# Two-layer diffusion backbone, one core: the token rows that layer 0 dispatches to its experts are transposed back from the modulated channels

## What is computed

```python
def modln(x, g, shift, scale):
    return rmsnorm(x, g) * (1 + scale) + shift
...
for l in range(DEPTH):                                  # DEPTH = 2
    sh_a, sc_a, gt_a, sh_f, sc_f, gt_f = jnp.split(mod, 6, axis=-1)   # mod = silu(c) @ w_mod[l] + b_mod[l]
    ...                                                 # attention part, x = x + gt_a * y
    h2 = modln(x, g_ffn[l], sh_f, sc_f)
    if need_ctx:                                        # layer 0: 512 tokens, layer 1: 256
        ...
        yt = hier_moe(toks, w_rg[l], b_rg[l], w_re[l], b_re[l], w_e_gate[l], w_e_up[l], w_e_down[l])
return rmsnorm(x, g_final)
```

## Time and profile before

| | us |
|---|---|
| median of 3 runs | 1371.19 (1368.15 to 1374.7) |
| the profiled execution, own time | 1368.83 |
| its span | 1366.6 |
| PE / DVE / ACT / POOL busy in the span | 1220.4 / 661.0 / 437.8 / 176.2 |
| mean granted clock of PE, share of full speed | 0.97 |
| router stage of layer 0, mod(0,5) to the first expert matmul | 474.6 to 526.6 |
| router stage of layer 1, the same | 1081.1 to 1117.0 |

### The profile page before, as it was taken

One profiled execution on the slowest core, in us unless ns is written; L12 is line 12 of the kernel. 1 busy time (PEld: TensorE's weight loads), 2 busy tenths in 40 slices (PEclk: granted clock), 3 DMA queues, 4 the chain that ended last, 5 costly groups with the idle time before them and its releaser, 6 DMA issues.

```text
span 1366.6 us, 22075 instructions
## 1 busy us (share of the span) xinstructions
PE 1220.4 (89%) x8916; PEld 930.6 (68%) x8916; DVE 661.0 (48%) x1506; ACT 437.8 (32%) x1028; POOL 176.2 (13%) x220
## 2 busy tenths in 40 slices
PE   4899888899998978899999789998998968889986
PEld 2788754688887947666666459865998845555652
DVE  1544686455346375422221285567767554233334
ACT  3533366433334440000100264346666510000001
POOL 1810000111013200100010311000101200000001
PEclk9999999999999989999999989999999889999997
DMA  9994145423324378999999995238565869999994
GB/s 353 318 353 144 62 152 188 125 93 93 95 90 185 114 270 346 360 418 415 407 388 375 403 222 158 101 131 280 161 184 184 321 255 418 418 416 415 387 373 168
DMA packets 132391, 353.26 MB, mean 258 GB/s; under 512 B 23214, under 2 KB 84902, under 8 KB 109121
## 3 DMA queue, kind: packets, MB, share of 16 engines
q1 hardware_dynamic: 118144, 317.69, 62.9%
q0 software_dynamic: 13008, 32.48, 6.9%
q10 hardware_dynamic: 1136, 1.66, 0.3%
HBM read 332.62 MB, written 28.88 MB: 265 GB/s over the span
## 4 chain that ended last, share of the span: by engine, by line
PE 78%; DVE 10%; issue 4%; DMA 4%; ACT 2%; POOL 0%; SPq 0%; DVEq 0%; POOLq 0%; ACTq 0%
PE banks L1030 33%; PE banks L1259 15%; PE banks L1273 8%; PE banks L1251 6%; PE banks L1198 4%; PE banks L967 2%; PE banks L1126 2%; PE banks L1141 2%; PE banks L1111 1%; DMA expert_rows<-arena,rows_u 1%; DMA ring<-in_w_in 1%; DMA ring<-in_w_mod 1%; PE banks L1223 1%; DVE arena L2387 1%; DVE arena L2355 1%
## 5 line engine op out<-in xcount | busy, mean ns | idle before, releaser
L2000 DVE TENSOR_TENSOR w_lo_r<-ring,w_hi_r 128x256 fp32r<-128x256 f32 x480 | 222.8, 474 | 239.9 <-ACT w_hi_r L1608 238.8
L1608 ACT ACTIVATE w_hi_r<-ring 128x256 fp32r<-128x256 f32 x480 | 197.4, 416 | 303.1 <-PE banks L1030 254.0
L1259 PE MATMUL banks<-ring,arena 128*64 128x256 f32 x2016 | 230.6, 381 | 28.1 <-issue 11.4
L1030 PE MATMUL banks<-h_hi_r,w_hi_r 128*128 128x512 f32 (+1 forms) x640 | 222.0, 347 | 6.5 <-DVE h_lo_r L1930 5.1
L1259 PEld LDWEIGHTS banks<-ring,arena 128*64 128x64 f32 x2016 | 161.3, 137 | 87.1 <-issue 36.1
L1030 PE MATMUL banks<-h_lo_r,w_hi_r 128*128 128x512 f32 (+1 forms) x640 | 220.4, 344 | 0.0
L1030 PE MATMUL banks<-h_hi_r,w_lo_r 128*128 128x512 f32 (+1 forms) x640 | 220.3, 344 | 0.0
L1030 PEld LDWEIGHTS banks<-h_hi_r,w_hi_r 128*128 128x128 f32 x640 | 123.0, 192 | 22.5 <-ACT arena L1578 5.0
L1030 PEld LDWEIGHTS banks<-h_hi_r,w_lo_r 128*128 128x128 f32 x640 | 122.9, 192 | 14.1
L1030 PEld LDWEIGHTS banks<-h_lo_r,w_hi_r 128*128 128x128 f32 x640 | 123.1, 192 | 13.8
L1273 PE MATMUL banks<-ring,att 128*64 128x512 f32 x424 | 119.4, 604 | 14.7 <-DVE att L2372 7.4
(11 more groups left out here) (269 smaller groups left out, 1734.2 us busy)
## 6 DMA issues: line engine op xcount, KB each, us to landing
ring<-in_w_e_gate SPq DMA_DIRECT2D x64, 1024.0 KB, 9.0
ring<-in_w_e_up SPq DMA_DIRECT2D x62, 1024.0 KB, 9.3
ring<-in_w_e_down SPq DMA_DIRECT2D x53, 1024.0 KB, 9.5
ring<-in_w_mod SPq DMA_DIRECT2D x48, 1024.0 KB, 6.3
ring<-in_w_in SPq DMA_DIRECT2D x38, 1024.0 KB, 5.5
expert_rows<-att POOLq DMA_DIRECT2D x23, 512.0 KB, 20.4
ring<-in_w_o SPq DMA_DIRECT2D x8, 1024.0 KB, 5.2
ring<-in_w_branch SPq DMA_DIRECT2D x8, 640.0 KB, 4.5
```

The source lines that it names most:

```text
L1030: ins = mm(out_ap, a, b, start=k == 0 and p_ == 0, stop=k == KD - 1 and p_ == 2)
L1259: ins = mm(banks[e * CAP:(e + 1) * CAP, bank, 0:DE], x[:, k, e * CAP:(e + 1) * CAP], w[:, k * DE:(k + 1) * DE], start=k == 0, stop=k == KD ...
L1608: fn(w_hi[:, u % AHEAD, :, :], chunk(key)[:, q * KU:(q + 1) * KU, :], ACT.Copy).then_inc(w_hi_ready, 1)
L2000: v.tensor_tensor(w_lo[:, u % AHEAD, :, :], chunk(key)[:, q * KU:(q + 1) * KU, :], w_hi[:, u % AHEAD, :, :].bitcast(F32), ALU.subtract).th ...
```

## The change

Six edits, all in the router stages and at the end:
1. Layer 0's second computation of the modulated rows goes away, with its four row stores, four broadcasts and DVE's two passes. PE transposes `hT` back instead (`turn_rows`: 8 transposes a tile; tiles 0 and 1 before mod(1,1), tiles 2 and 3 after `ranks`), and ACT copies each tile out twice (`htok`, `th_hi`). `hT` moves to tiles 0 to 7 of `arena`. Rows now have `hT`'s channel order, so `rest_rows` reads without stride.
2. `ffn_norm` on DVE does the statistics before mod_add(0,5) and before the column copies, which now stand in the middle of the scaling.
3. The router product is done in two halves: even blocks into PSUM partitions 0 to 35, odd ones into 64 to 99. ACT copies one, DVE the other; PE adds both while turning them, by matmuls with the identity.
4. `ranks` signals after the ranks and again after the counts, which get a bank of their own.
5. mod_add(1,1) stands ahead of `place`, mod_add(1,0) between two halves of `rest_rows`.
6. At the end the tiles go through RMSNorm one by one, and tile 1 is stored in two halves.

```diff
-        hT = [att[:, NTOK * k:NTOK * (k + 1)] for k in range(KD)]
+        hT = [arena[:, k, :] for k in range(KD)]
...
+        ROW_BANKS = [(3, 0), (4, 5), (3, 0), (4, 5)]
...
-                if l == 0:
-                    rows_out(0, 4)
-                    rows_out(0, 3)
                 merge(l)
-                if l == 0:
-                    pool.wait_ge(branch_done, 24)
-                    rows_in(0, 4, mod_scale, ffn_rows_in)
-                    rows_in(0, 3, mod_shift, ffn_rows_in)
...
-                    ins = mm(banks[0:NR, 0, 0:n], w_router[:, k, :], hT[k][:, 0:n], start=k == 0, stop=k == KD - 1)
+                    p0 = k % 2 * 64
+                    ins = mm(banks[p0:p0 + NR, 0, 0:n], w_router[:, k, :], hT[k][:, 0:n], start=k < 2, stop=k >= KD - 2)
                 ins.then_inc(lgT_done, 1)
                 pe.wait_ge(lgT_out, l + 1)
-                hold()
+                pe.wait_ge(lgT_out_dve, l + 1)
                 for tt in range(QT[l]):
-                    ins = turn(banks[:, 2, tt * NR:(tt + 1) * NR], lgT[:, tt * P:(tt + 1) * P], ident[0:NR, 0:NR])
+                    for half in range(2):
+                        ins = mm(banks[:, 2, tt * NR:(tt + 1) * NR], lgT[half][:, tt * P:(tt + 1) * P], ident[0:NR, 0:NR],
+                                 start=half == 0, stop=half == 1)
...
+            def turn_rows(tiles):
+
+                for tt in tiles:
+                    if tt >= 2:
+                        pe.wait_ge(th_hi_ready, tt - 1)
+                    for k in range(KD):
+                        ins = turn(banks[:, ROW_BANKS[tt][k // 4], k % 4 * P:(k % 4 + 1) * P], hT[k][:, tt * P:(tt + 1) * P], ident)
+                    ins.then_inc(h_rows, 1)
...
                 for u in range(1, nt):
-                    mm(banks[:, 1, u * NE:nt * NE], C["ones"], pairs[:, 0:(nt - u) * NE], start=False, stop=u == nt - 1)
+                    ins = mm(banks[:, 1, u * NE:nt * NE], C["ones"], pairs[:, 0:(nt - u) * NE], start=False, stop=u == nt - 1)
+                ins.then_inc(rank_done, 1)
                 for u in range(nt):
-                    ins = mm(banks[:, 1, 4 * NE:5 * NE], C["ones"], both[:, u, :], start=u == 0, stop=u == nt - 1)
+                    ins = mm(banks[:, 2, 8 * NE:9 * NE], C["ones"], both[:, u, :], start=u == 0, stop=u == nt - 1)
                 ins.then_inc(rank_done, 1)
...
                 pe.wait_ge(sel_ready, n + 1)
+                if l == 0:
+                    pe.wait_ge(th_hi_ready, 3)
...
+                    if l == 0:
+                        for tt in (2 * r, 2 * r + 1):
+                            act.wait_ge(h_rows, tt + 1)
+                            for dst in (htok[:, tt, :], th_hi[:, tt, :]):
+                                for half, b in enumerate(ROW_BANKS[tt]):
+                                    ins = fn(dst[:, half * 512:half * 512 + 512], banks[:, b, :], ACT.Copy)
+                            ins.then_inc(th_hi_ready, 1)
-                if l == 0:
-                    act.wait_ge(wo_done, 4 * nt)
-                    for tt in range(nt):
-                        act.wait_ge(h_rows, tt + 1)
-                        fn(th_hi[:, tt, :].rearrange("p (k s) -> p k s", k=KD),
-                           htok[:, tt, :].rearrange("p (s k) -> p k s", k=KD), ACT.Copy).then_inc(th_hi_ready, 1)
...
                 residual(l)
-                mod_add(*MOD_ROUTE[l][0])
                 ffn_norm(l)
                 if l:
-                    rest_rows(1)
+                    rest_rows(1, range(2))
                 route(l)
                 if l == 0:
-                    shift_rows()
+                    mod_add(*MOD_ROUTE[0][1])
                 place(l, False)
-                for k, sec in MOD_ROUTE[l][1:]:
-                    mod_add(k, sec)
                 if l == 0:
-                    rest_rows(0)
+                    rest_rows(0, range(2))
+                    mod_add(*MOD_ROUTE[0][2])
+                    rest_rows(0, range(2, 4))
...
+            for c in range(2):
+                gathered_row(0, c)
+            add_own(1, 0)
+            gathered_row(1, 0)
+            mean_square(2, 0)
+            gathered_row(1, 1)
+            add_own(1, 1)
             dve.wait_ge(g_in, 16)
+            final_scale(0)
+            mean_square(2, 1)
+            final_scale(1)
```

More of the change, by code:

```diff
@@ L361, in program @@
         g_col = sb("g_col", [P, DEPTH, KD])
-        mod_scale = [tile(0, 2), tile(4, 2)]
-        mod_shift = [tile(2, 2), tile(6, 2)]
         gate_bc = [gate_t[:, s, :] for s in range(2)]
@@ L407, in program @@
         g8 = att[:, 1280:1312].rearrange("p (t e) -> p t e", t=4)
-        lgT = att[0:NR, 3072:3072 + NTOK]
+        lgT = [att[0:NR, 3072 + NTOK * half:3072 + NTOK * (half + 1)] for half in range(2)]
         rope_t = att[:, 2304:2304 + 4 * SEQ].rearrange("p (a b) -> p a b", a=4)
@@ L1498, in _ @@
                 route(l)
+                if l == 0:
+                    turn_rows((0, 1))
                 for k, sec in MOD_ROUTE[l][1:2]:
@@ L1502, in _ @@
                 ranks(l)
+                if l == 0:
+                    turn_rows((2, 3))
                 for k, sec in MOD_ROUTE[l][2:]:
@@ L1710, in route @@
                 act.wait_ge(lgT_done, l + 1)
-                fn(lgT[:, 0:QN[l]], banks[0:NR, 0, 0:QN[l]], ACT.Copy).then_inc(lgT_out, 1)
+                fn(lgT[0][:, 0:QN[l]], banks[0:NR, 0, 0:QN[l]], ACT.Copy).then_inc(lgT_out, 1)
                 for r, (dst, src) in enumerate((
@@ L1845, in _ @@
                 fn(htok[:, tt, :], X[:, tt, :], ACT.Square, accum_out=stat[:, tt:tt + 1]).then_inc(sq_done, 1)
-            act.wait_ge(ms_ready, MS0[4] + 1)
-            fn(stat[:, 8:12], stat[:, 4:8], ACT.Sqrt).then_inc(std_ready, 1)
-            for tt in range(2):
-                act.wait_ge(fin_ready, tt + 1)
-                act.dma_start(out[0, tt * P:(tt + 1) * P, :], htok[:, tt, :]).then_inc(stored, 16)
-            act.wait_ge(stored, 32)
+                act.wait_ge(ms_ready, MS0[4] + tt + 1)
+                fn(stat[:, 8 + tt:9 + tt], stat[:, 4 + tt:5 + tt], ACT.Sqrt).then_inc(std_ready, 1)
+            act.wait_ge(fin_ready, 1)
+            act.dma_start(out[0, 0:P, :], htok[:, 0, :]).then_inc(stored, 16)
+            for half in range(2):
+                at = slice(512 * half, 512 * half + 512)
+                act.wait_ge(fin_ready, 2 + half)
+                act.dma_start(out[0, P:2 * P, at], htok[:, 1, at]).then_inc(stored, 16)
+            act.wait_ge(stored, 48)
         @block.vector
@@ L1955, in ffn_norm @@
                 v.reciprocal(stat[:, 12:16], stat[:, 8:12]).then_inc(f_rstd_ready, 1)
+                mod_add(*MOD_ROUTE[l][0])
                 dve.wait_ge(f_rstd_ready, l + 1)
                 for tt in range(nt):
+                    if tt == nt // 2:
+                        for n, (dst, bank) in enumerate(((f_mul, 6), (f_add, 7))):
+                            dve.wait_ge(f_cols_done, 2 * l + n + 1)
+                            v.tensor_copy(dst[:, :, :], banks[:, bank, 0:2 * KD].rearrange("p (k s) -> p k s", s=2))\
+                                .then_inc(f_col_ready, 1)
                     r = stat[:, 12 + tt:13 + tt]
@@ L1972, in ffn_norm, with rest_rows @@
                                         ALU.mult, ALU.add).then_inc(hT_dve, 1)
[L1973 to L1994 removed]
+            def rest_rows(l, tiles):
+                for tt in tiles:
+                    dve.wait_ge(th_hi_ready, QT0[l] + tt + 1)
+                    v.tensor_tensor(th_lo[:, tt, :], htok[:, tt, :], th_hi[:, tt, :].bitcast(F32), ALU.subtract).then_inc(th_lo_ready, 1)
             def split_w(key, q):
@@ L2166, in route @@
                 nt = QT[l]
+                dve.wait_ge(lgT_done, l + 1)
+                v.tensor_copy(lgT[1][:, 0:QN[l]], banks[64:64 + NR, 0, 0:QN[l]]).then_inc(lgT_out_dve, 1)
+                link(v.memset(g8[:, :, :], NEG))
                 dve.wait_ge(lg_done, l + 1)
-                link(v.memset(g8[:, :, :], NEG))
                 link(v.tensor_tensor(lg[:, 0:nt, :], banks[:, 2, 0:nt * NR].rearrange("p (t n) -> p t n", t=nt),
```

70 lines of the change are left out of this document (21 added, 49 removed).

## The result

| | before | changed |
|---|---|---|
| median, us | 1370.37 (14 runs) | 1363.46 (14 runs, 1359.36 to 1366.49) |
| ratio to before | 1 | 0.9945, 95% interval [0.993, 0.9959] |
| profiled execution, own time / span | 1368.83 / 1366.6 | 1366.03 / 1364.2 |
| router stage of layer 0: mod(0,5) to the first expert matmul | 52.0 | 42.7 |
| router stage of layer 1, the same | 35.9 | 37.9 |

The change is 6.9 us faster by the medians, 7.5 by the ratio (5.6 to 9.6 by its interval). The forecast was 11.7 won, at 1359.5. Everything ahead of mod(0,5), which the change leaves alone, took 2.16 us longer in it than in the profile before (476.75 against 474.59).

The account below looks back on a forecast made before the run. Bounds: PE, 78% of the chain, with gains where the chain leaves PE; layer 0's weight stream second. Terms 7.2 + 3.5 + 1.0 = 11.7 us gave 1359.5 from the median, own range 1355 to 1363, wider range 1353 to 1366.

Parts of the forecast that it names:

- Layer 0, 7.2: Layer 0's router stage and weight stream: 7.2 us won, taken between 6.7 and 7.6.
- Statistics first: Layer 0, before the router product: transposes wait only for the column copy, start 482.4 for 483.88, 1.5 us won.
- halves side by side: Layer 0's router product: two halves run two by two, 0.22 us a pass, ending at 491.7; 5.1 us won so far.
- the queue's next request: Layer 0's weight queue: next piece asked for at 522.7 instead of 530.33, data at 524.6 for 531.3, 6.7 us won.
- Layer 1, 3.5: Layer 1's router stage: earlier transposes and product, ranks not waiting for counts; 3.5 us won, bounds 2.5 and 4.5.
- Before they were hidden under the product, now they are late next: Layer 1: `th_hi` (2.01 us) and `rest_rows` (2.36) stand ahead of the router result's copies; DVE's copy at 1094.2.
- The end, 1.0: Final norm and store: last half row ready 0.7 us earlier, last store half as long; 1.0 us, bounds 0.4 and 1.6.
- Clock rival: Layer 0, router product to mod(1,1): clock falls to 1.2 GHz, layer 0 wins 3.7 us, time 1363; chance 0.15.
- Halves don't overlap: Router product still takes 7.0 us; layer 0 wins 3.7, layer 1 3.2, time 1363.3; chance 0.10.
- stream eats it: Weight waits up to 670 return all of layer 0's gain but 1.9 us; time 1364.8; chance 0.08.
- slower: PE stays at 1.2 GHz from router product to dispatch, layer 0 9.2 us late; time 1375.9; chance 0.04.
- Dispatch released by ACT's `th_hi`: Layer 0: ACT's 16 copies arrive last, ending tile 3 at 508.5; dispatch starts then instead of 514.58.

Follow-up runs that it names:

- two repeats: Changed kernel with 100 and 160 empty PE instructions, which the build dropped, so byte for byte the changed kernel; ratios to before 0.993 and 0.9931.
- l0_only: Changed kernel with its edits of layer 1 and of the end undone; ratio to before 0.9947, 7.3 us faster.
- pad100: Changed kernel plus 25 thin matmuls (100 instructions) at the first unit of layer 1's output projection; ratio to before 0.9938.
- pad200: Changed kernel plus 50 thin matmuls (200 instructions) at the first unit of layer 1's output projection; ratio to before 0.9916.
- pad200_copy: pad200 with layer 1's copies of the router result ahead of `th_hi` and th_lo, `rest_rows` behind `place`; ratio to before 0.989, median 1356.24 us.
- pad256: Changed kernel plus 64 thin matmuls (256 instructions, a whole block) at the first unit of layer 1's output projection; ratio to before 0.9925.
- tail_only: Kernel before with only edit 6, the norm tile by tile and last store in halves; ratio to before 0.9993, 1.0 us faster.
- before_pad: Kernel before plus 38 thin matmuls in layer 0's output projection and 26 in layer 1's; ratio to before 0.9994.
- turn_later: pad_both with layer 0's first 16 `turn_rows` transposes moved behind mod(1,1); ratio to before 0.9875.
- pad_both: pad200_copy, but with 38 thin matmuls in layer 0's output projection and 12 in layer 1's; ratio to before 0.9904.

## Why the forecast came out as it did

- **Sum.** 11.7 forecast, 6.9 measured (7.5 by the ratio; 9.6 and 9.5 in the two repeats). The measured time (1363.46) is in the range of 1353 to 1366, but 0.5 above the forecast's own range of 1355 to 1363. The number is in range by luck in part: one term of three, layer 1, brought nothing, and the range was wide enough for it.
- **Layer 0, 7.2: right.** l0_only gives 7.3. Statistics first, halves side by side, the memset ahead of the signal, `place` without `shift_rows` and the queue's next request all show as forecast. Inside, two sizes were off. The stage gained more: eight profiles with the same layer 0 code (the changed kernel, its two repeats, l0_only, pad100, pad200, pad200_copy, pad256) have 42.7 to 44.4, mean 43.4, against 52.0 and 52.1 for before and tail_only: 8.7 us, 7.6 forecast. The forecast had DVE pace the router product; in fact PE's own passes pace it (0.43 us each in either half), and it ends at 492.62, which is 490.5 on the axis of before, 1.2 ahead of the 491.7 forecast. And the kernel lost some behind the stage: the first expert's matmuls take 8.8 us, at a clock of 0.50 in part, in nine of the eleven profiles with the changed layer 0, and 7.13 in the three without. What lies between the first expert and mod(1,5) varies from 554.4 to 561.1 us over the profiles, so the rest of the difference can't be followed there.
- **Layer 1, 3.5: the term that failed.** "Now they start at 1087.0 ... The same edits let the product end at about 1092": the first half was right, and then came a wait that I had not named, for PE's own instructions. Against 35.88 (before), 34.99 (tail_only) and 35.84 (before_pad), mean 35.6, the four profiles with the gap in its old place have 37.94, 35.79, 36.30 and 35.60, mean 36.4: nothing won, some 0.8 us lost, which is within the spread of the single stages. With the code moved so that nothing is awaited, the stage is 32.7 (one profile, pad200) and 2.9 us are won, within my bounds of 2.5 to 4.5. There DVE's copy ends 13.2 us after mod(1,5) begins; the forecast's 1094.2 is 13.1. So the working was sound and the code's position took its gain away. A sign of such a wait stood in the earlier trace rows, PE's 1.66 us of idle time marked issue among the columns; the working gave it no term. "Before they were hidden under the product, now they are late next" was right as well: taking `th_hi` and `rest_rows` out of the way makes the stage another 2.4 us shorter.
- **The end, 1.0: as forecast** (tail_only 1.0; DVE's last row 0.9 earlier), but the interval of tail_only takes in no gain at all.
- **Clock rival (0.15).** It came in part. The changed kernel's windows from 496 to 500 have 0.62, 0.50, 0.50, 0.67; `turn_rows` took 2.88 and mod(1,1) 4.37. Of the ten profiles that have `turn_rows` ahead of mod(1,1), six have 1.97 and 3.66, four 2.66 to 2.95 and 4.29 to 4.59. It costs 1.6 us when it comes (0.9 and 0.7), not the 4 that I gave it; in turn_later mod(1,1) alone lost 1.7. The Trainium skill's rule (its page "TensorE: Matmul & The Clock Gate", Part 4), that the full clock does not engage for transposes, is too strong for this kernel: in the changed profile 32 transposes ran at 1.00 throughout. But its direction is seen: in pad200 the clock fell from 1.00 to 0.53 while PE did nothing but transposes (2.70 us for 16). Which of the two happens I can't tell from these rows.
- **Halves don't overlap (0.10), stream eats it (0.08), slower (0.04):** not seen; the weight queue had no pause ahead of 524.87 (share 0.92 to 1.08 in the windows from 519). "Dispatch released by ACT's `th_hi`" was a near miss: ACT ended at 509.42, mod(1,0) left PE free at the same time, and the dispatch began at 509.74.
- The best versions are those with the code moved and layer 1's copies first: 0.989 (pad200_copy), 0.9904 (pad_both), 0.9875 (turn_later), where the change alone has 0.9945, 0.993 and 0.9931. That is 13 to 17 us, for the change's 7 to 10; among the three the intervals don't choose.

## What to carry to other kernels

When an edit moves code on an engine with cheap instructions, ask what the engine's own program costs to fetch, and look in the trace for gaps marked "issue" that stand at the same instruction whatever the data do. A gap of that kind moves with the code ahead of it, so two kernels that differ by 88 instructions ahead of a stage can differ in it though nobody touched it (35.9 and 37.4 us here, 0.8 of it the gap itself); compare stages, and place the block's end in a wait that is there anyway. And an early product is worth only what the queues behind it let through: reorder the copies in the same edit. Run the same kernel again before you explain a miss: here its two repeats won 2 us more than the first measurement.

## What the runs showed of the hardware

- A PE program block of 256 instructions came late. Gaps of 0.79 to 4.27 us in the stage of layer 1 (seven profiles), of 1.52 to 1.85 in layer 0 (eleven), each ending 1.2 to 1.5 us after an instruction packet of 16 KB had landed (packet from 1085.66 to 1086.69, PE again at 1088.04). In the changed kernel PE passed the end of the block before (15069) at about 1080.2 and got the new one 7.8 us later. The weight queue ran at a share of 1.0 in the gap; that its load makes the block late was not tried, only the block's end and its period were.
- The column products do 128 passes in 2.1 us, 256 instructions. Code of this kind is the densest in the kernel (elsewhere 256 recorded instructions take over 6 us), and there, or just behind it, the block ran out.
- Two products of 36 rows, in partitions 0 to 35 and 64 to 99, run side by side: each keeps its 0.43 us a pass of 512 columns, and together 16 passes take 3.73 us for 7.03.
- Empty PE instructions don't move code, since the build drops them (layer 1's columns begin at PE's record 14,800 with and without). Thin matmuls do, at 1.74 us for 25 of them and 5.44 us for 64. From the first expert to mod(1,5) pad256, with its 64, takes 557.3 us as the changed kernel does (557.2), so they are hidden behind DVE's work there.
- With the same code up to there, layer 0's 32 transposes took 3.81, 3.83, 5.10, 5.42, 5.43, 6.10, 6.14 and 6.17 us in the eight profiles: the granted clock there differs from run to run. The stages differ by 1.6 us, less than the transposes, since those that were fast there were slow behind (`turn_rows` 2.88 and 2.95 where the transposes took 3.81 and 3.83).
